# Sums of the routed experts kept by feature: y stationary, a placing matrix of 304 columns moving, and sums in place of x until the layer norm

## What is computed

```
wts = top 8 of 64 experts per token, from sigmoid scores      # (T, 8)
per expert e, over the rows of its tokens:
    hb  = silu(xb @ w_gate[e]) * (xb @ w_up[e])               # 1024 -> 256
    acc[toks] += (hb @ w_down[e]) * gates                     # 256 -> 1024
moe = acc + (silu(x @ sh_gate) * (x @ sh_up)) @ sh_down
x   = layer_norm(ALPHA * x + moe)
```

## Time and profile before

| | |
|---|---|
| time, median of 3 executions | 1428.08 us (1427.16 to 1428.22) |
| profiled execution, time | 1424.99 us |
| profiled execution, span | 1423.2 us |
| mean granted clock of TensorE | 0.982 |
| TensorE busy | 1357.8 us (95%) |
| VectorE busy | 613.1 us (43%) |
| ScalarE busy | 345.0 us (24%) |
| GpSimd busy | 51.3 us (4%) |
| DMA | 435.51 MB, mean 306 GB/s |
| scatter matmuls (L824) | 792 of 512 columns |
| adds to x (L1575) | 396 of 512 elements |

### The profile page before, as it was taken

One profiled execution on the slowest core, in us unless ns is written; L12 is line 12 of the kernel. 1 busy time (PEld: TensorE's weight loads), 2 busy tenths in 40 slices (PEclk: granted clock), 3 DMA queues, 4 the chain that ended last, 5 costly groups with the idle time before them and its releaser, 6 DMA issues.

```text
span 1423.2 us, 17890 instructions
## 1 busy us (share of the span) xinstructions
PE 1357.8 (95%) x6574; PEld 708.1 (50%) x6574; DVE 613.1 (43%) x1194; ACT 345.0 (24%) x690; POOL 51.3 (4%) x96
## 2 busy tenths in 40 slices
PE   6989989999999999999999689999999999999994
PEld 4555546544444544445544565444454444554442
DVE  0766256343434343334343774333434333343336
ACT  1633321222212222222222132222222212222221
POOL 6100000000000000000000200000000000000000
PEclk9999999999999999999999979999999999999997
DMA  9421028699989989998998424999899989989961
GB/s 275 117 83 42 34 82 316 236 389 389 386 362 393 390 343 421 395 371 360 411 392 343 160 90 173 368 388 375 358 410 390 390 358 396 388 342 422 395 273 33
DMA packets 72102, 435.51 MB, mean 306 GB/s; under 512 B 12915, under 2 KB 15075, under 8 KB 22016
## 3 DMA queue, kind: packets, MB, share of 16 engines
q1 hardware_dynamic: 69248, 428.13, 75.6%
q0 software_dynamic: 2816, 6.87, 1.6%
HBM read 433.23 MB, written 1.76 MB: 306 GB/s over the span
## 4 chain that ended last, share of the span: by engine, by line
PE 92%; DVE 4%; ACT 1%; issue 1%; DMA 1%; SPq 0%; DVEq 0%
PE bank L882 32%; PE bank L798 19%; PE bank L830 16%; PE bank L824 13%; PE bank L782 3%; PE bank L1198 3%; PE bank L892 1%; PE bank L989 1%; PE bank L952 1%; DVE sb_x L1646 1%; DVE sb_ln_st L1638 1%; DVE sb_x L1642 1%; DMA sb_x<-in_x_sample_dram 1%; DVE sb_att L1748 0%; PE bank L1278 0%
## 5 line engine op out<-in xcount | busy, mean ns | idle before, releaser
L1575 DVE TENSOR_TENSOR sb_x<-sb_x,bank 128x512 f32<-128x512 f32 (+1 forms) x396 | 242.1, 679 | 118.6 <-PE bank L824 118.6
L830 PE MATMUL bank<-sb_wslot,sb_ht 128*64 128x512 f32 x1024 | 231.0, 593 | 0.0
L882 PE MATMUL bank<-sb_wslot,sb_xg_own 128*64 128x512 f32 x1024 | 226.5, 595 | 1.7 <-ACT sb_xg_own L1330 1.7
L882 PE MATMUL bank<-sb_wslot,sb_xt 128*64 128x512 f32 x1024 | 226.8, 595 | 0.0
L1594 DVE TENSOR_TENSOR sb_hh<-sb_sg,bank 128x256 f32<-128x256 f32 x64 | 27.0, 421 | 375.5 <-ACT sb_sg L1354 375.5
L1581 DVE SCALAR_TENSOR_TENSOR sb_yl<-bank,sb_gslot,sb_yh 128x512 fp32r<-128x512 f32 x128 | 96.1, 751 | 162.8 <-ACT sb_yh L1336 162.8
L798 PE MATMUL bank<-sb_pick,sb_xh 128*128 128x512 f32 x432 | 160.8, 401 | 0.0
L824 PE MATMUL bank<-sb_yh,sb_place 128*128 128x512 f32 x396 | 157.5, 398 | 3.3 <-DVE sb_yl L1581 3.3
L1354 ACT ACTIVATE sb_sg<-bank 128x256 f32<-128x256 f32 x64 | 24.6, 384 | 550.1 <-PE bank L882 550.1
L824 PE MATMUL bank<-sb_yl,sb_place 128*128 128x512 f32 x396 | 156.6, 395 | 0.0
L830 PEld LDWEIGHTS bank<-sb_wslot,sb_ht 128*64 128x64 f32 x1024 | 72.8, 137 | 144.6 <-issue 139.3
(11 more groups left out here) (304 smaller groups left out, 1047.2 us busy)
## 6 DMA issues: line engine op xcount, KB each, us to landing
sb_wslot<-in_moe_w_gate_dram SPq DMA_DIRECT2D x64, 2048.0 KB, 8.0
sb_wslot<-in_moe_w_up_dram SPq DMA_DIRECT2D x64, 2048.0 KB, 12.8
sb_wslot<-in_moe_w_down_dram SPq DMA_DIRECT2D x64, 2048.0 KB, 15.0
sb_w_in_hi<-in_w_in_dram SPq DMA_DIRECT2D x2, 2048.0 KB, 14.6
sb_w_in_lo<-in_w_out_dram SPq DMA_DIRECT2D x1, 4096.0 KB, 12.6
sb_w_in_lo<-in_w_in_dram SPq DMA_DIRECT2D x2, 1024.0 KB, 11.2
sb_ln_g<-in_ln_g_dram POOLq DMA_DIRECT2D x4, 512.0 KB, 4.8
sb_ln_b<-in_ln_b_dram POOLq DMA_DIRECT2D x4, 512.0 KB, 6.0
```

Source lines behind the costliest of these rows:

```text
L830: last = pe.matmul(y_b[c][64 * e:64 * e + 64, :], ht[:, k, 64 * e:64 * e + 64], w_down[u][:, e, k * D + c * 512:k * D + (c + 1) * 512], st ...
L882: last = pe.matmul(gu_b[64 * e:64 * e + 64, :], xgt[b][:, k, sl], w_gu[u][:, :, e, k * FE:(k + 1) * FE], start=k == 0, stop=k == DK_SLICES ...
L1575: dve.tensor_tensor(dst, dst, banks.tile[order[f]][0:rows, :], ALU.add).then_inc(s["added"], 1)
```

## The change

Sums are kept by feature. `acc` is a view of the memory of `x`: 8 slices of 304 tokens on 128 partitions. In the scatter 128 features of `yh` or `yl`, every eighth, are stationary and the 304 used columns of the placing matrix move: eight sums instead of six, each of 304 columns. `spread`, from which L892 makes the placing matrix, gets its identity columns packed, so that the tokens of the third tile stand in columns 256 to 303. The shared expert's down projection is made by feature slices too, and ALPHA times `xt` plus it starts `acc`. After the last scatter, `sums_to_tokens` transposes the sums back to rows of tokens in six banks, and `norm_sums` takes the norm's statistics and the first operation from these banks, writing `x` in the natural order of features. The bank orders get longer, the waits follow, and GpSimd's load of the cached rows waits for the first normed tile.

```diff
-FILLS = 2 * TILES
-SUM_BANKS = (7, 4, 5, 6, 7, 4)
-LAST_SUM_BANKS = (4, 5, 7, 6, 5, 7)
+FILLS = DK_SLICES
+SUM_BANKS = (7, 4, 5, 6, 7, 4, 5, 6)
+LAST_SUM_BANKS = (4, 5, 7, 6, 7, 6, 7, 6)
+END_SUM_BANKS = (7, 4, 5, 6, 2, 3, 0, 1)
+TOKENS = N_PROMPT + N_DEC
...
-        u += [("sd", l, t, c) for t in range(TILES) for c in range(2)]
+        u += [("sd", l, f) for f in range(DK_SLICES)]
+        u += [("fx", l, t, c) for t in range(TILES) for c in range(2)]
...
+        acc = x[:, :, :].rearrange("p t d -> p (t d)")[:, 0:DK_SLICES * TOKENS].rearrange("p (k n) -> p k n", n=TOKENS)
...
                 if l:
+                    gp.wait_ge(x_ready, 4)
                     gp.dma_start(x[CACHE_ROW:CACHE_ROW + 15, 2, :], a["cache_pool"][0]).then_inc(s["pool_c_in"], 16)
...
-            def place_add(u, i, order):
+            def place_add(u, i, order, copies):
 
                 pe.wait_ge(s["y_ready"], 2 * i + 1)
                 pe.wait_ge(s["place_copied"], i + 1)
                 for f in range(FILLS):
-                    t, c = divmod(f, 2)
-                    if order[f] == 6:
-                        pe.wait_ge(s["place_copied"], i + 2)
-                        pe.wait_ge(s["gate_ready"], 2 * i + 3)
+                    if order[f] == 6 and 6 not in order[:f]:
+                        pe.wait_ge(s["place_copied"], copies + 1)
+                        pe.wait_ge(s["gate_ready"], 2 * copies + 1)
                     if order[f] in order[:f]:
-                        pe.wait_ge(s["added"], FILLS * i + order[:f].index(order[f]) + 2)
+                        before = max(k for k in range(f) if order[k] == order[f])
+                        pe.wait_ge(s["added"], FILLS * i + before + 2)
                     for h, part in enumerate((yh, yl)):
-                        last = pe.matmul(banks.tile[order[f]][:, :], place[u][:, t * P:(t + 1) * P],
-                                         part[:, c * 512:(c + 1) * 512], start=h == 0, stop=h == 1)
+                        last = pe.matmul(banks.tile[order[f]][:, 0:TOKENS], part[:, f::DK_SLICES], place[u][:, 0:TOKENS],
+                                         start=h == 0, stop=h == 1)
                     last.then_inc(s["sum_done"], 1)
+
+            def sums_to_tokens(total):
+
+                for t in range(TILES):
+                    for c in range(2):
+                        name = ("fx", l, t, c)
+                        f = max(END_SUM_BANKS.index(banks.at[name][0]), 4 * c + 3)
+                        pe.wait_ge(s["added"], FILLS * total + f + 2)
+                        ps = banks.open(pe, name)
+                        for k in range(4):
+                            src, cols = acc[:, 4 * c + k, :], slice(k * P, (k + 1) * P)
+                            if t < 2:
+                                last = transpose(pe, ps[:, cols], src[:, t * P:(t + 1) * P])
+                            else:
+                                pe.matmul(ps[0:32, cols], src[:, 2 * P:2 * P + 32], ident, start=True, stop=True)
+                                last = pe.matmul(ps[32:64, cols], src[:, TOKENS - N_DEC:TOKENS], ident, start=True, stop=True)
+                        last.then_inc(banks.fill_sem(name), 1)
...
                         if m == BODY - 1:
                             pe.wait_ge(s["added"], FILLS * i + 2)
-                            down_pair(u, i, n, FILLS * i + 6)
+                            down_pair(u, i, n, FILLS * i + 3)
             total = rounds * PAIRS
             pe.wait_ge(s["added"], FILLS * total + 1)
-            place_add(1, total, (7, 4, 5, 2, 3, 0))
+            place_add(1, total, END_SUM_BANKS, total)
+            sums_to_tokens(total)
...
                 def shared_down():
                     for b in range(2):
                         banks.copied(pe, ("su", l, b))
-                    token_products("sd", l, lambda k, tc: sh_h[:, k, tc], sh_down, 2)
+                    for f in range(DK_SLICES):
+                        stage(("sd", l, f), lambda ps: accumulate(pe, ps[:, 0:T_COLS], [
+                            (sh_down[:, k, f::DK_SLICES], sh_h[:, k, :]) for k in range(2)]))
...
             def add_sums(i, order):
                 for f in range(FILLS):
-                    t, c = divmod(f, 2)
-                    rows = ROWS[t]
-                    dst = x[0:rows, t, c * 512:(c + 1) * 512]
                     dve.wait_ge(s["sum_done"], FILLS * i + f + 1)
-                    dve.tensor_tensor(dst, dst, banks.tile[order[f]][0:rows, :], ALU.add).then_inc(s["added"], 1)
+                    dve.tensor_tensor(acc[:, f, :], acc[:, f, :], banks.tile[order[f]][:, 0:TOKENS], ALU.add).then_inc(s["added"], 1)
...
+            def norm_sums(l):
+
+                n = 2 * l + 1
+                for t in range(TILES):
+                    rows = ROWS[t]
+                    xr = x[0:rows, t, :]
+                    for c in range(2):
+                        ps = banks.full(dve, ("fx", l, t, c))
+                        step(dve.bn_stats(ln_st[0:rows, t, c, :], ps[0:rows, :]))
+                    step(dve.bn_aggr(ln_mv[0:rows, t, :], ln_st[0:rows, t, :, :].rearrange("p a b -> p (a b)")), var_ready)
+                    if t == 0:
+                        dve.wait_ge(ln_in, 32 * (n + 1))
+                        for t2 in range(TILES):
+                            for c in range(2):
+                                banks.full(dve, ("fx", l, t2, c))
+                    for c in range(2):
+                        by_f = lambda ap: ap.rearrange("p (q f) -> p f q", f=DK_SLICES)[:, 4 * c:4 * c + 4, :]
+                        ps = banks.ap(("fx", l, t, c))[0:rows, :].rearrange("p (f q) -> p f q", f=4)
+                        step.banked(dve.scalar_tensor_tensor(out=by_f(xr), in0=ps, scalar=ln_mv[0:rows, t, 0:1], in1=by_f(ln_g[0:rows, :]),
+                                                             op0=ALU.subtract, op1=ALU.mult), banks, ("fx", l, t, c))
...
-                for t in range(TILES):
-                    rows = ROWS[t]
-                    for c in range(2):
-                        n, xr = ("sd", l, t, c), x[0:rows, t, c * 512:(c + 1) * 512]
-                        ps = banks.full(dve, n)
-                        step.banked(dve.scalar_tensor_tensor(out=xr, in0=xr, scalar=ALPHA, in1=ps[second(t, c), :],
-                                                             op0=ALU.mult, op1=ALU.add), banks, n)
+                if l:
+                    dve.wait_ge(s["pool_c_in"], 16)
+                for f in range(DK_SLICES):
+                    ps = banks.full(dve, ("sd", l, f))
+                    for c0, c1, q0 in ((0, N_PROMPT, 0), (N_PROMPT, TOKENS, SAMPLE0)):
+                        cols = slice(q0, q0 + c1 - c0)
+                        ins = dve.scalar_tensor_tensor(out=acc[:, f, c0:c1], in0=xt[:, f, cols], scalar=ALPHA, in1=ps[:, cols],
+                                                       op0=ALU.mult, op1=ALU.add)
+                    ins.then_inc(banks.empty_sem(("sd", l, f)), 1)
...
-                layer_norm(2 * l + 1, lambda t, rows: None)
+                norm_sums(l)
```

More of the change, by code:

```diff
@@ L589, in sp_experts @@
             load_pair(sp, l, 1, 1, DN)
-            banks.full(sp, ("sd", l, TILES - 1, 1))
+            banks.full(sp, ("sd", l, DK_SLICES - 1))
             load_pair(sp, l, 1, 1, GU[:1])
@@ L859, in pe_experts @@
             for b in (2, 3):
-                banks.freed(pe, b, ("sd", l, TILES - 1, 1))
+                banks.freed(pe, b, ("sd", l, DK_SLICES - 1))
             for kk in range(DK_SLICES):
@@ L864, in pe_experts @@
                 gather(0, kk)
-            banks.all_copied(pe, ("sd", l, TILES - 1, 1))
+            banks.all_copied(pe, ("sd", l, DK_SLICES - 1))
             pe.wait_ge(s["init"], 5 - l)
@@ L899, in pe_experts @@
                             gather(1 - b, 2 * q + c)
-                        place_add(1 - u, i, LAST_SUM_BANKS if m == BODY - 1 else SUM_BANKS)
+                        place_add(1 - u, i, LAST_SUM_BANKS if m == BODY - 1 else SUM_BANKS, i + 1)
                         if m == 0:
@@ L1548, in _ @@
                         act.activation(spread[:, b, 0:2, 0:P], bc(ident, 1, 2), ACT.Copy)
-                        ins = act.activation(spread[0:64, b, 2, 0:P], ident[0:64, :], ACT.Copy)
+                        act.activation(spread[0:32, b, 2, 0:TAIL], ident[0:32, 0:TAIL], ACT.Copy)
+                        ins = act.activation(spread[32:64, b, 2, TAIL:TAIL + N_DEC], ident[32:64, 32:64], ACT.Copy)
                     ins.then_inc(s["w_ready"], 1)
@@ L1608, in dve_experts @@
                 dve.wait_ge(s["next_round"], r + 1)
-            add_sums(PAIRS * rounds, (7, 4, 5, 2, 3, 0))
+            add_sums(PAIRS * rounds, END_SUM_BANKS)
             dve.wait_ge(s["added"], FILLS * (PAIRS * rounds + 1) + 1)
@@ L1643, in layer_norm @@
                                                   op0=ALU.subtract, op1=ALU.mult))
+                    dve.wait_ge(sd_ready, 3 * n + t + 1)
```

(5 more changed lines are left out.)

## The result

The changed kernel takes **1506.89 us** (median of 5 executions, 1503.86 to 1509.16) against 1428.08 (1424.95 to 1428.79): ratio 1.0561, 95% interval 1.0545 to 1.0577. The forecast was 1427.9 with a range up to 1446. It was wrong. The profiled execution took 1503.86 us with a span of 1502.1.

What follows compares the result with a forecast made beforehand. TensorE's queue was taken as the bound (92% of the chain of waits). Terms of -12, +4, +0.7, +4.2 and +3.3 us were summed to -0.2, set against the median 1428.08: 1427.9 us, range 1414 to 1446.

Steps and rivals of the forecast that it cites:

- Part 4: Scatter's weight loads of y at stride eight: at most 0.12 us each, hidden behind the 0.145 us matmuls, costing nothing.
- Rival (a): Scatter's strided stationary loads take 0.18 to 0.22 us and set the pace: total 1442 to 1464 us; chance 0.14.
- Part 1: Scatter matmuls: 16 of 304 columns replace 12 of 512, 0.145 us each instead of 0.232; block 2.32 us without waits.
- Part 2: Scatter adds on VectorE, 0.386 us apart, make TensorE wait for banks: 0.21 us saved per pair, -12 us in 56 pairs.
- Part 3: Last pair of each body: five sums follow each other in two banks, 3.79 us instead of 3.26, +4 us in 8 bodies.
- Parts 5 to 7: Start of the experts +0.7 us; end of layer and its norm +4.2 us in layer 1, +3.3 us in layer 0.
- part 6: End of a layer: sums return to rows through TensorE, norm may write x after 7.35 us instead of about 6.1.
- part 7: Last norm: strided halves take 1.1 us, a tile 1.0 us more; VectorE and GpSimd exclude each other on the second port.

Runs made afterwards that it cites:

- e1: The changed kernel with each slice of y taken as contiguous columns instead of every eighth, features in another order: 1426.77 us, ratio 1.0008.
- e8: e7 with each add over 152 of the 304 columns, half of the tokens' sums left out: 1390.61 us (one execution).
- e7: e6 with the last pair's sums in four banks in turn, the next down projection waiting for later sums: 1415.91 us, ratio 0.9929.
- e5: e1 with the moving w_down read every eighth element, which puts the features in order: 1673.76 us, ratio 1.1753.
- e6: e1 with the features sorted in ScalarE's and VectorE's copies from bank to y: 1425.59 us, ratio 1.0004.
- e4: The changed kernel, y still strided, with only 128 of the 304 columns moving, other tokens' sums left out: 1525.93 us (one execution).

## Why the prediction was wrong

**Part 4 failed**, the step "eight loads in 0.97 us, at most 0.12 each ... so the loads stay hidden and cost nothing". As a ceiling for a transpose's load the 0.12 is right: these loads, of 185 to 207 ns in their records, do start 0.11 us apart. The step that does not hold is carrying the ceiling over from the transposes to the ordinary products of the scatter, where the same stride gives loads of 336 ns and matmuls 0.244 us apart (e1 without the stride: 187 ns, 0.139). The spacing also hides that the transposes' loads pay at all, since contiguous ones stand as close: the 16 at the changed kernel's end take 1.97 us. What tells it is the loads' own length. The transposes' weight loads (L782) of the kernel before, min/median/max ns, first the two tiles read with a stride (two and eight elements), then a contiguous one, and last the eight of the earlier trace rows alone:

```profile
L782 PEld LDWEIGHTS bank<-sb_cst,sb_hh x128: 194/198/219, 269.7 to 1390.7; 128*128 128x128 f32 x128
L782 PEld LDWEIGHTS bank<-sb_cst,sb_x x72: 182/203/231, 10.9 to 829.8; 128*128 128x128 f32 x48, 64*128 64x128 f32 x24
...
L782 PEld LDWEIGHTS bank<-sb_cst,sb_og x12: 136/140/142, 171.2 to 179.7; 128*128 128x128 f32 x8, 64*128 64x128 f32 x4
...
L782 PEld LDWEIGHTS bank<-sb_cst,sb_x x8: 185/194/207, 204.5 to 205.3; 128*128 128x128 f32 x8
```

203 against 140 ns stood in the trace before the change: a sign that a strided load pays, which I did not read. It would not have given the size. The price in an ordinary product is larger still, as the changed kernel shows beside the scatter in the shared expert, first its down projection with a stationary stride of eight, then its gate and up products with one of two:

```profile
L803 PEld LDWEIGHTS bank<-sb_xg_own,sb_wslot x32: 312/313/334, 240.0 to 248.3; 128*128 128x128 f32 x32
L803 PEld LDWEIGHTS bank<-sb_xt,sb_wslot x11: 195/197/197, 235.9 to 238.6; 128*128 128x128 f32 x11
```

There the 313 ns hide behind 0.27 us of moving columns; behind 0.139 they can't. A record is longer than what the load costs in a row: 336 ns go with a distance of 0.244, 330 with 0.233. Why a transpose's load is cheaper is left open, and the transposes differ in a second way, left open too: stride 2 costs them as much as stride 8 (198 and 203 against 140), where ordinary loads pay for it only from four.

**Rival (a) was right and undersized.** It took 0.18 to 0.22 per load from twice the transposes' 0.11, which was itself a spacing; the loads are 0.244 apart. By its own working, 0.24 gives a block of 3.9 and the +68 us found. Its chance of 0.14 was too low: two rows spoke for it (VectorE's at this stride, and the loads' lengths above, unread), and the one row against it was of transposes and did not carry over. The range left it out beyond 1446.

**Part 1 held** once the load was out of the way: 0.139 for 0.145 (e1). **Part 2 held**: adds 0.381 apart for 0.386, the first 0.48 after the block's start for 0.49, block 2.62 for 2.67, and e8 shows that the adds and not the matmuls bound it. A middle pair gains 0.26 (16.34 to 16.08) for 0.21. **Part 3 held**: 3.73 for 3.79; the last pair's block is 0.47 longer than before for 0.53, and e7 shows the two banks to be the reason. Together the 64 pairs of e1 are 10.6 us shorter, forecast 7.6 (the windows of the loops, with the last scatters, 11.6).

**Parts 5 to 7 held.** The start of the experts and the end of layer 1 in the changed kernel, timeline:

```profile
240.02 8.98 PE L803 MATMUL bank<-sb_xg_own,sb_wslot 128*128 128x320 f32 x32 [0.69 <-issue]
...
1475.50 0.54 PE L829 MATMUL bank<-sb_place,sb_yh 128*128 128x304 f32 x1 [1.65 <-DVE sb_yl L1604]
...
1480.22 1.97 PE L787 MATMUL bank<-sb_cst,sb_x 128*128 128x128 f32 x16 [0.56 <-DVE sb_x L1598]
1480.98 1.43 DVE L1680 BATCH_NORM_STATS2 sb_ln_st<-bank 128x6 f32<-128x512 f32 x2 [0.82 <-PE bank L787]
...
1484.20 2.30 DVE L1690 SCALAR_TENSOR_TENSOR sb_x<-bank,sb_ln_mv,sb_ln_g 128x512 f32<-128x512 f32 x2 [1.54 <-PE bank L847]
...
1486.73 1.28 DVE L1694 SCALAR_TENSOR_TENSOR sb_x<-sb_x,sb_ln_rs,sb_ln_b 128x1024 f32<-128x1024 f32 x1
...
1492.30 1.28 DVE L1694 SCALAR_TENSOR_TENSOR sb_x<-sb_x,sb_ln_rs,sb_ln_b 128x1024 f32<-128x1024 f32 x1
```

32 records of the shared down projection take 8.98 us (forecast 8.6 and the tail). From its start to the gather pass 9.70 us in e1 and in the changed kernel and 8.90 before: +0.8, forecast +0.7. A half of the strided operation takes 1.15 (1.1), a tile 1492.30 - 1486.73 = 5.57 (5.53), VectorE waits 1.54 for the banks (1.7). From the last scatter's first matmul to the end are 1502.1 - 1475.5 = 26.6 us, in e1 25.6 and before 21.0: without the stride +4.6, forecast +4.2.

The end of layer 0 in e1:

```profile
781.12 0.41 PE L829 MATMUL bank<-sb_place,sb_yh 128*128 128x304 f32 x1 [1.65 <-DVE sb_yl L1604]
...
788.45 2.30 DVE L1690 SCALAR_TENSOR_TENSOR sb_x<-bank,sb_ln_mv,sb_ln_g 128x512 f32<-128x512 f32 x2 [1.84 <-PE bank L847]
...
793.18 4.71 POOL L758 TENSOR_TENSOR sb_wslot<-sb_wslot 128x1024 f32<-128x1024 f32 x2
...
796.63 2.34 DVE L1694 SCALAR_TENSOR_TENSOR sb_x<-sb_x,sb_ln_rs,sb_ln_b 128x1024 f32<-128x1024 f32 x1
```

The first strided operation starts 7.33 us after the last scatter's first matmul (part 6: 7.35). The second tile is normed at 796.63 + 2.34 - 781.12 = 17.85, before at 15.0: +2.9, forecast +3.3. GpSimd's product holds up one operation beside tile 1 by 1.1 us (1.5). The Trainium skill's rule on the second port, named in part 7, had no experiment, but these rows agree with it as the 2.77 did: the operation with two SBUF inputs (L1694) takes 2.34 for 1.28 beside the product, the one that reads a bank and one SBUF input (L1690) 2.39 for 2.30.

**The sum.** It was added wrongly: -11.8 + 4.2 + 0.7 + 4.2 + 3.3 is +0.6 and not -0.2, which moves the forecast to 1428.7 and changes no reading. (In part 2, 0.60 - 0.217 is 0.383; by the slope of the earlier trace rows the 0.217 is 0.211, and 0.387 comes out; measured 0.381.) In the profiled execution of e1 the changed parts add up to -10.6 + 0.8 + 2.9 + 4.6 = -2.3. Its span is still 2.6 longer than the span before, since 4.9 us lie where the forecast has no term: 2.1 ahead of the shared down projection and 2.8 between the second tile's norm and the next loop.

These stretches differ from one execution to another: e5, with the same code in them, is 0.6 and 1.4 us shorter there than the kernel before. The whole stretch between the layers, in the same instructions, takes 96.0 us at a mean granted clock of 0.86 in e1, 90.8 at 0.91 in the changed kernel and 90.1 at 0.92 in e8: the differences of 5 and 6 us are those in time lost to the clock (0.14 x 96.0 = 13.4, 0.09 x 90.8 = 8.2, 0.08 x 90.1 = 7.2, estimates from these windows). So a total near the forecast's in e1 is in part luck: the pairs gained 3 us more than forecast, and the clock of this execution took it back.

## What to carry to other kernels

Before an operand changes places between moving and stationary, look at the stride in which the new stationary is read: at strides of four and eight fp32 elements such loads of 128 columns set a pace of 0.233 and 0.244 us here, as much as 512 moving fp32r columns (0.232). The distance of matmuls shows only the longer of load and moving columns; whether a load pays for its stride, its own length tells. Neither carries over from a transpose to an ordinary product: what a load costs in a row was seen only where nothing hid it, and it was less than its record (0.244 us against 336 ns). And put a permutation where an engine with time to spare reads a bank anyway: here ScalarE's and VectorE's copies did it for nothing. A sum that returns to a bank should find the longest possible turn of banks: that order alone was worth 9 us, where the whole change without the slow loads was worth nothing measurable (e6).

## What was not expected of the hardware

- A weight load of 128 by 128 fp32 values takes 187 to 190 ns contiguous, 194 to 196 at stride 2, 330 at 4, 336 at 8 beside fp32r products, and successive products with a slow load stand 0.233 to 0.244 us apart. A transpose's load takes 140 contiguous, 198 at stride 2, 203 at 8.
- A moving fp32 operand at stride 8 doubles its product: mean 593 to 1096 ns, +3.9 us in a pair (e5).
- ScalarE's and VectorE's reads of a bank at stride 8, written in runs of 64, cost nothing (688 and 751 ns, e6).
- With fewer moving columns in the scatter the granted clock over the loops was 0.98 and not 1.00, and pairs of 18.92 us stood among those of 17.22 (e4, one execution; the cause was not tested).
- The same instructions between the layers take 90 to 96 us by the granted clock (0.92 to 0.86). One kernel's executions differ too: the six of e7 take 1411.79 to 1419.07 us, at a mean clock of 0.985 and 0.979.
- A VectorE operation with two SBUF inputs takes 2.34 us for 1.28 beside GpSimd's product; one with a bank and one SBUF input 2.39 for 2.30 (e1).
